# S5 tables: the rotations move from VectorE to GpSimd, and three of the four store streams change the engine that sends them

## The reference, cut to what matters

```python
lam_re = jnp.minimum(A_re, -1e-4); lam_im = A_im; dt = jnp.exp(log_dt)[:, None]
mag = jnp.exp(lam_re * dt)
ab_re, ab_im = mag * jnp.cos(lam_im * dt), mag * jnp.sin(lam_im * dt)   # one step of the state
...
_, _, st_re, st_im = lax.associative_scan(_cplx_op, (a_re, a_im, bu_re, bu_im), axis=1)
y = einsum('gcn,bsgn->bsgc', C_re, st_re) - einsum('gcn,bsgn->bsgc', C_im, st_im)
```

```python
def conv_ffn(xn, w_up, conv_w, conv_b, w_down):
    h = causal_dwconv(xn @ w_up, conv_w, conv_b)
    gate, val = jnp.split(h, 2, axis=-1)
    return (jax.nn.silu(gate) * val) @ w_down
```

## Time and profile before

| | |
|---|---|
| time, median of 3 runs | 2796.97 us (2796.58 to 2798.2) |
| the profiled execution's own time | 2796.79 us |
| its span in the trace | 2795.1 us |
| PE busy / DVE / ACT / POOL | 2632.7 / 1346.1 / 930.6 / 822.1 us |
| table building, group 1 | about 1177 to 1278 us |
| table building, group 2 | about 1386 to 1486 us |

### The profile page before, as it was taken

How to read it: one execution, slowest core, us unless ns; L and a number is a source line. 1 busy time by engine, 2 the same in 40 slices (tenths; PEclk the granted TensorE clock), 3 DMA queues, 4 the chain that set the end, 5 groups by cost and what they waited for, 6 DMA issues and landing times.

```text
span 2795.1 us, 35824 instructions
## 1 busy us (share of the span) xinstructions
PE 2632.7 (94%) x13567; PEld 2186.4 (78%) x13567; DVE 1346.1 (48%) x1668; ACT 930.6 (33%) x1420; POOL 822.1 (29%) x685
## 2 busy tenths in 40 slices
PE   6999799999699999989989999969999999999998
PEld 5778588877587887778778888958878888888886
DVE  5441376776434555674674445642334413431443
ACT  3442354544433312233233344322232312321333
POOL 4222233342322222362362221132222222222221
PEclk8999899999899999999999999989999999999998
DMA  2111000000012211142142124631111111111112
GB/s 90 42 45 49 16 1 1 1 1 1 16 52 57 57 45 49 49 151 95 49 153 92 45 76 154 212 98 49 49 42 49 45 52 46 49 49 49 49 45 83
DMA packets 239923, 164.57 MB, mean 59 GB/s; under 512 B 23981, under 2 KB 227271, under 8 KB 237767
## 3 DMA queue, kind: packets, MB, share of 16 engines
q1 hardware_dynamic: 227648, 149.76, 17.7%
q10 hardware_dynamic: 12167, 13.35, 1.4%
HBM read 129.51 MB, written 29.36 MB: 57 GB/s over the span
## 4 chain that ended last, share of the span: by engine, by line
PE 55%; issue 8%; DVE 4%; POOL 3%; DMA 2%; ACT 1%; ACTq 0%; POOLq 0%; SPq 0%; DVEq 0%
PE acc_o L1556 48%; PE acc_o L1805 3%; POOL dense_lo L374 2%; DMA s_states<-t_hx 2%; DVE t_hx L2430 1%; PE bank_b L2719 1%; PE bank_a L2696 1%; DVE t_tmp L2224 1%; DVE t_rot L2224 0%; POOL c_lo L2560 0%; DVE val L2040 0%; POOL t_mg L2376 0%; DVE t_rot L2407 0%; DVE t_rot L2406 0%; PE acc_o L2108 0%
## 5 line engine op out<-in xcount | busy, mean ns | idle before, releaser
L374 POOL TENSOR_TENSOR dense_lo<-dense_raw,dense_hi 128x512 fp32r<-128x512 f32 x324 | 428.0, 1321 | 1274.2 <-ACT dense_hi L367 1272.9
L367 ACT CAST dense_hi<-dense_raw 128x512 fp32r<-128x512 f32 x324 | 191.4, 593 | 765.5 <-PE acc_o L1556 713.3
L1556 PE MATMUL acc_o<-a_hi,dense_hi 128*128 128x512 f32 x1328 | 414.6, 393 | 8.2 <-POOL a_lo L2566 4.6
L1556 PE MATMUL acc_o<-a_lo,dense_hi 128*128 128x512 f32 x1328 | 410.8, 391 | 0.0
L1556 PE MATMUL acc_o<-a_hi,dense_lo 128*128 128x512 f32 x1328 | 410.4, 390 | 0.0
L1556 PE MATMUL acc_o<-c_hi,dense_hi 128*128 128x512 f32 x1096 | 341.1, 392 | 26.7 <-POOL dense_lo L374 24.5
L1556 PE MATMUL acc_o<-c_lo,dense_hi 128*128 128x512 f32 x1096 | 338.4, 390 | 0.0
L1556 PE MATMUL acc_o<-c_hi,dense_lo 128*128 128x512 f32 x1096 | 338.1, 390 | 0.0
L1556 PEld LDWEIGHTS acc_o<-a_hi,dense_hi 128*128 128x128 f32 x1328 | 248.3, 189 | 61.3 <-POOL a_lo L2566 5.8
L1556 PEld LDWEIGHTS acc_o<-a_lo,dense_hi 128*128 128x128 f32 x1328 | 250.7, 189 | 52.7
L1556 PEld LDWEIGHTS acc_o<-a_hi,dense_lo 128*128 128x128 f32 x1328 | 250.4, 189 | 52.3
(11 more groups left out here) (382 smaller groups left out, 3778.2 us busy)
## 6 DMA issues: line engine op xcount, KB each, us to landing
dense_raw<-in_f_w_up SPq DMA_DIRECT2D x176, 256.0 KB, 3.0
dense_raw<-in_f_w_down SPq DMA_DIRECT2D x72, 256.0 KB, 2.9
w_raw_e<-in_e_w_in SPq DMA_DIRECT2D x44, 256.0 KB, 2.9
s_states<-t_hx ACTq DMA_DIRECT2D x16, 512.0 KB, 3.9
g_in<-s_inputs SPq DMA_DIRECT2D x8, 1024.0 KB, 5.2
hx<-s_states SPq DMA_DIRECT2D x8, 1024.0 KB, 5.3
dense_raw<-in_o_w_glu SPq DMA_DIRECT2D x32, 256.0 KB, 2.8
s_inputs<-t_in SPq DMA_DIRECT2D x14, 512.0 KB, 3.9
```

Of the source, the lines that this page charges most:

```text
L367: nc.scalar.copy(self.hi[:, par, 0:n, :], self.raw[:, par, 0:n, :]).then_inc(w_hi_done, 1)
L374: pool.tensor_tensor(self.lo[:, par, 0:n, :], self.raw[:, par, 0:n, :], self.hi[:, par, 0:n, :].bitcast(F32), op=ALU.subtract).then_inc(w_ ...
L1556: last = nc.tensor.matmul(acc[:, h * HALF:(h + 1) * HALF], w[:, chunk, j, :], x[:, k + j, h * HALF:(h + 1) * HALF], start=first, stop=final)
```

## The change

Rotations are made by POOL (`turns_pool`), one after each up unit of tiles 1 to 4 of groups 1 and 2, into two buffers in turn. SP sends them behind the weight loads of the units that follow. ACT sends the input tables and filters at the end of `half_act`. DVE keeps `t_hx` and `t_mh`. The same transfers of the same sizes are made; `t_tmp` and the second `t_rot` lie elsewhere in SBUF.

```diff
         def load_sp(self, sp):
-            def keep(g, c):
-                n0 = (g - 1) * DT
-                if 0 <= c - 4 < DT:
-                    self.tables.keep_filters_sp(sp, n0 + c - 4)
...
-                elif self.builds(g - 1):
-                    for m in range(2):
+                elif self.builds(g):
+                    for m in range(n):
                         for half in range(2):
                             self.load_up(sp, g, m, half)
-                            keep(g - 1, DT + 2 * m + half)
...
+                            if m > 1:
+                                self.tables.keep_turns_sp(sp, (g - 1) * DT + 2 * m - 4 + half)
...
                 if self.builds(g):
-                    for c in range(2, DT):
-                        self.dn.load(sp, w, n, bass.ds(c * P, P), self.down_unit(g) + c, 0)
-                        keep(g, c)
...
+                    for half in range(2):
+                        self.tables.keep_turns_sp(sp, (g - 1) * DT + DT - 2 + half)
...
         def lo_pool(self, pool):
...
+                if self.builds(g):
+                    for m in range(1 if self.builds(g - 1) else 0, n):
+                        for half in range(2):
+                            self.dn.take_lo(pool, DT, m * 2 + (self.up_unit(g) + half), 0)
+                            if m:
+                                self.tables.turns_pool(pool, (g - 1) * DT + 2 * m - 2 + half)
...
                         if m == n - 1 and self.builds(g):
-                            self.tables.turns_dve(dve, n0)
                             self.tables.powers_dve(dve, n0)
...
-    t_rot = at("t_rot", [P, 2, 2, N5], X_AT)
+    t_rot = [at(f"t_rot{s}", [P, 2, 2, N5], where) for s, where in enumerate((X_AT, Z_AT))]
...
             if n % DT < DT - 1:
                 self.powers_dve(dve, n + 1)
-                self.turns_dve(dve, n + 1)
...
+        def turns_pool(self, pool, n):
...
+            if n == 0:
+                pool.wait_ge(s5_clear, 23)
+            if n > 1:
+                pool.wait_ge(t_turns_out[n % 2], 16 * (n // 2))
+            for o, a, b in ((turn[0], cos, far_cos), (tmp[0], sin, far_sin), (turn[1], sin, far_cos), (tmp[1], cos, far_sin)):
+                pool.tensor_tensor(o, a, b, op=ALU.mult).then_inc(t_turned, 1)
+            pool.wait_ge(t_turned, 6 * n + 4)
+            pool.tensor_tensor(turn[0], turn[0], tmp[0], op=ALU.subtract).then_inc(t_turned, 1)
+            pool.tensor_tensor(turn[1], turn[1], tmp[1], op=ALU.add).then_inc(t_turned, 1)
+            pool.wait_ge(t_turned, 6 * n + 6)
+
+        def keep_turns_sp(self, sp, n):
+            i, two = n // 2, slice(2 * (n % 2), 2 * (n % 2) + 2)
+            sp.wait_ge(t_turned, 6 * n + 6)
+            sp.dma_start(d_turns[i, :, two, :], t_rot[n % 2][:, :, :, :].rearrange("p q k n -> p q (k n)")).then_inc(t_turns_out[n % 2], 16)
...
         def states_dve(self, dve, n):
             if n:
                 dve.wait_ge(t_pe, 4 * n)
-                dve.wait_ge(t_states_out, 32 * n)
+                dve.wait_ge(t_states_out, 16 * n)
...
             nc.scalar.copy(t_fir[:, :, 1, :], self.k1[:, :, :]).then_inc(t_kept, 1)
+            self.keep_filters(act, n)
...
-            act.dma_start(d_turns[i, :, two, :], t_rot[:, :, :, :].rearrange("p q k n -> p q (k n)")).then_inc(t_states_out, 16)
...
+        def keep_filters(self, act, n):
             i, two = n // 2, slice(2 * (n % 2), 2 * (n % 2) + 2)
-            sp.wait_ge(t_kept, 11 * n + 11)
...
+            act.wait_ge(t_kept, 11 * n + 11)
+            act.dma_start(d_inputs[i, :, two, :], self.inputs(n)[:, :, :]).then_inc(t_filters_out, 16)
+            act.dma_start(d_filters[i, :, two, :], t_fir[:, :, :, :].rearrange("p q a n -> p q (a n)")).then_inc(t_filters_out, 16)
```

More of the change, by code:

```diff
@@ L1841, in load_sp @@
                 if self.builds(g):
-                    for c in range(2, DT):
-                        self.dn.load(sp, w, n, bass.ds(c * P, P), self.down_unit(g) + c, 0)
-                        keep(g, c)
[L1845 to L1848, removed]
+                    for half in range(2):
+                        self.tables.keep_turns_sp(sp, (g - 1) * DT + DT - 2 + half)
+                with sp.Fori(1, DT // 2) as i:
+                    for s in range(2):
+                        self.dn.load(sp, w, n, bass.ds(i * (2 * P) + s * P, P), i * 2 + (self.down_unit(g) + s), 0)
         def lo_pool(self, pool):
@@ L1855, in lo_pool @@
                     self.dn.take_lo(pool, DT, self.up_unit(g) + 1, 0)
-                with pool.Fori(1 if self.builds(g - 1) else 0, n) as m:
-                    for half in range(2):
-                        self.dn.take_lo(pool, DT, m * 2 + (self.up_unit(g) + half), 0)
+                if self.builds(g):
[4 more added lines that the diff above has]
+                                self.tables.turns_pool(pool, (g - 1) * DT + 2 * m - 2 + half)
+                else:
+                    with pool.Fori(1 if self.builds(g - 1) else 0, n) as m:
+                        for half in range(2):
+                            self.dn.take_lo(pool, DT, m * 2 + (self.up_unit(g) + half), 0)
                 self.pair_lo(pool, g, 0)
@@ L2130, in trunk @@
     c_s5 = at("c_s5", [P, 2, S5_PAIRS, 16], X_AT + 2 * TILE)
-    t_tmp = at("t_tmp", [P, 2, 2, N5], Z_AT)
+    t_tmp = at("t_tmp", [P, 2, 2, N5], E_AT + 4992)
     t_fir = at("t_fir", [P, 2, 2, P], Z_AT + 2048)
@@ L2155, in trunk @@
     s_act, s_arg, c_kept = sem("s_act"), sem("s_arg"), sem("c_kept")
-    t_pool, t_dve, t_pe, t_kept, t_states_out, t_filters_out = (
-        sem("t_" + n) for n in "pool dve pe kept states_out filters_out".split())
+    t_pool, t_dve, t_pe, t_kept, t_states_out, t_filters_out, t_turned = (
+        sem("t_" + n) for n in "pool dve pe kept states_out filters_out turned".split())
+    t_turns_out = [sem(f"t_turns_out{s}") for s in range(2)]
     V = {n: small[:, k, :] for k, n in enumerate(
@@ L2399, in turns_dve @@
             far_cos, far_sin = (coarse[:, k, pr, :].unsqueeze(3).to_broadcast(step) for k in range(2))
-            turn = [t_rot[:, :, k, :].rearrange("p q (a b) -> p q a b", b=16) for k in range(2)]
+            turn = [t_rot[n % 2][:, :, k, :].rearrange("p q (a b) -> p q a b", b=16) for k in range(2)]
             tmp = [t_tmp[:, k, :, :].rearrange("p q (a b) -> p q a b", b=16) for k in range(2)]
-            if n:
-                dve.wait_ge(t_states_out, 32 * n)
[L2404 to L2407, removed]
+            if n == 0:
[12 more added lines that the diff above has]
+            sp.dma_start(d_turns[i, :, two, :], t_rot[n % 2][:, :, :, :].rearrange("p q k n -> p q (k n)")).then_inc(t_turns_out[n % 2], 16)
         def powers_dve(self, dve, n):
@@ L2491, in keep_states @@
             act.wait_ge(t_dve, 4 * n + 4)
[L2492 removed]
             act.dma_start(d_states[i, :, two, :].rearrange("p q (a x) -> p (q a) x", a=2),
                           t_hx[:, :, :, 1:K9, :].rearrange("p q a k c -> p (q a) (k c)")).then_inc(t_states_out, 16)
[L2496 removed]
+        def keep_filters(self, act, n):
             i, two = n // 2, slice(2 * (n % 2), 2 * (n % 2) + 2)
[L2498 to L2500 removed]
+            act.wait_ge(t_kept, 11 * n + 11)
+            act.dma_start(d_inputs[i, :, two, :], self.inputs(n)[:, :, :]).then_inc(t_filters_out, 16)
+            act.dma_start(d_filters[i, :, two, :], t_fir[:, :, :, :].rearrange("p q a n -> p q (a n)")).then_inc(t_filters_out, 16)
         def wait_kept(self, eng, n):
[L2504 removed]
+            eng.wait_ge(t_states_out, 16 * n)
             eng.wait_ge(t_filters_out, 32 * n)
@@ L2618, in _ @@
                 dn.wait_unit(sp, u_in - 1, 1)
-                sp.wait_ge(t_states_out, 32 * HALVES)
+                sp.wait_ge(t_states_out, 16 * HALVES)
+                sp.wait_ge(t_turns_out[0], 8 * HALVES)
+                sp.wait_ge(t_turns_out[1], 8 * HALVES)
                 sp.wait_ge(t_filters_out, 32 * HALVES)
```

5 lines of the change are left out of this document (removed).

## The result

The changed kernel takes 2760.6 us, median of 4 runs (2760.0 to 2762.14), against 2797.48 us for the kernel before (4 runs, 2796.58 to 2798.2): a ratio of 0.9869, interval 0.9852 to 0.9886. The gain is 36.9 us, and the forecast was 2760.

What follows compares the result with a forecast made beforehand. PE bounds the kernel except in the two table stages, where it waits on a loop through DVE and a DMA landing. 17.7 + 16.5 + 2.6 - 0.5 = 36.3 us off 2796.8 gave 2760, range 2756 to 2772.

Steps and rivals of the forecast that it cites:

- table stage, group 1: Down projection of group 1: 19.4 us lost by PE, all but 1.7 taken back, 17.7 us.
- table stage, group 2: Down projection of group 2: 18.2 us lost by PE, all but 1.7 taken back, 16.5 us.
- start of the two down projections: Last up tile: without six rotations ahead of DVE's scale, PE's 1.3 us wait goes in each group, 2.6 us.
- meeting of POOL and DVE: Up projection, after gate units: rotations meet `val<-gate,val`, delaying POOL's subtraction; 0.5 us lost in all, bounds 0 and 3.4.
- The ring: Table stages: DVE's loop through `t_hx`, its landing and the rotations, 12 to 14 us, falls to 6.3 to 9.8.
- The turn at PE's own pace: Table stages: one unrestrained unit of five k tiles and its half takes PE 9.76 us.
- The first turn: Start of each table stage: stays at 11.48 us, 1.72 over, as POOL's table instructions precede the small subtraction.
- The landing of `t_hx`: Table stages: DMA landing of 3.2 to 5.8 us, within a loop that no longer binds, or barely.
- Rival 1: Table stages: the next ring binds through `t_hx`'s landing, turn 10.8 us, 2772; range 2766 to 2778, chance 0.26.
- ACT's two issues: Table stages: ACT sends input tables and filters, about 0.5 us each, covered by PE's unit; price zero.
- Rival 3: Up projection: rotations hold up `dense_lo` beyond 6.9 us; slower than before at 4.6 us a tile; chance 0.04, shared.
- The room of POOL in the table stage: Table stages: POOL's own work in a turn sums to 8.4 us, 9.3 at the longest, under PE's 9.76.

Runs made afterwards that it cites:

- R = 3: The changed kernel with POOL making the four products of each rotation three times, outputs unchanged: 2796.96 us, ratio 0.9998.
- R = 2: The changed kernel with POOL making the four products of each rotation twice, outputs unchanged: 2767.15 us, ratio 0.9891.

## Why the prediction was right

The two traces are laid side by side by the lag of after against before at the same instruction; its steps are the terms. The lag falls by 1.40 us at the start of the down projection of group 1 and by 17.78 in its table stage, (1275.19 - 1177.69) in the earlier trace rows less 1258.39 - 1178.67 here. Then by 1.35 and 16.59 in group 2, where after has 1368.71 and 1448.42. Below is PE's timeline of the changed kernel: first the start of the stage of group 2, then the first rows of the last half of either stage, which end the two stretches:

```profile
1368.71 0.47 PE L1556 MATMUL acc_o<-c_hi,dense_hi 128*128 128x512 f32 x1 [0.91 <-POOL dense_lo L374]
```

```profile
1258.39 0.38 PE L2449 MATMUL bank_a<-ident,t_gx 128*128 128x128 f32 x2
...
1448.42 0.27 PE L2449 MATMUL bank_a<-ident,t_gx 128*128 128x128 f32 x1
```

| term | predicted | measured |
|---|---|---|
| table stage, group 1 | 17.7 | 17.8 |
| table stage, group 2 | 16.5 | 16.6 |
| start of the two down projections | 2.6 | 2.75 |
| meeting of POOL and DVE | -0.5 | -0.3 at most |
| sum | 36.3 | 36.9 (medians; these rows sum to 36.8) |

- **The ring.** It was the landing of `t_hx` ahead of the rotations. The second buffer alone, with all work left on DVE, gave 27.2 us, so this is shown. The forecast did not say how the two parts of the cure divide: some three quarters are the wait, the rest comes with taking the work off DVE.
- **The turn at PE's own pace.** 9.76 us from one row of before, 9.74 in every turn after the first. The clock came back with the wait, as the windows show.
- **The first turn.** 11.48 us before and after, to the hundredth.
- **The landing of `t_hx`** was bounded by 3.2 to 5.8 us and is 3.0 in the median, 4.6 at most (2.9/3.0/4.6 from issue to landing). Rival 1 needed it long. It got shorter, since rotations are gone from its burst (with the tables back on SP it is 3.0 us as well), and there is spare time around it: DVE waits 1.66 us for PE ahead of `t_hx`.
- **POOL's `t_gx`** ends at 1200.40 + 3.59 = 1203.99, 4.1 us after PE begins the unit behind its half (1199.89), inside the 5 us that the forecast named as the limit.
- **Rotations on POOL** were taken at 4.0 us for six. The products take 0.62 us and the two sums 0.74. One rotation, the meeting and what comes of it, in the timelines of POOL and DVE:

```profile
1122.43 0.62 POOL L2405 TENSOR_TENSOR t_rot<-fine,coarse 128x256 f32<-128x256 f32 x1
...
1125.57 0.74 POOL L2408 TENSOR_TENSOR t_rot<-t_rot,t_tmp 128x256 f32<-128x256 f32 x1
...
1129.24 1.74 POOL L374 TENSOR_TENSOR dense_lo<-dense_raw,dense_hi 128x512 fp32r<-128x512 f32 x1 [2.93 <-ACT dense_hi L367]
```

```profile
1125.85 1.54 DVE L2050 TENSOR_TENSOR val<-gate,val 128x1024 f32<-128x1024 f32 x1
```

  The rotation ends at 1126.31, 3.9 us after it began. `val<-gate,val` takes 1.54 us where the earlier trace rows have 1.23: it was held up for 0.3 us by the rotation's last instruction, still running when it started. The subtraction then ends at 1130.98 and PE starts its unit at 1131.18 without idle time. The slack, 0.51 us in the earlier trace rows, is 0.20. The meeting that I priced at 0.5 us is there, is 0.3 us long, and the slack swallows it. The period of a tile is 21.79 us after and 21.76 before, by DVE's scales of two successive tiles, and 8 x 0.03 us is 0.24.
  By the Trainium skill, page "SBUF — State Buffer", section "Who interferes with whom", each excludes the other for a whole instruction. The rows agree that it works in both directions (`val<-gate,val` 1.54 us against 1.23, a product on POOL 1.60 against 0.62), but the strict price of 3.4 us was not paid, since only the last, short instruction of POOL was in the way.
- **ACT's two issues** cost nothing, as said, and not for the whole reason given. The unit on PE covers them, and with the rotations off the ring either sender will do. But the edit shortens the landing of `t_hx`, and on the kernel before this was worth 5 us. The forecast had weighed the issues' time and not what the transfers leave free.
- **Rival 3** was priced at 4.6 us a tile for a loss, six instructions in 11.5 us. The experiment with R = 3, 8.8 us undisturbed, already gave all of it back. So the room up to the crossing was over-priced: I had let PE pay a us for each us of POOL, and meetings with DVE and the clock after the waits come on top. With the two meetings those 8.8 us are 10.7, 3.8 over the 6.9 us of room, and the tile pays 5.0 for them. With R = 2 PE's waits rise by 13.0 - 7.2 = 5.8 us and the medians by 6.6: behind waits of 0.8 us the granted clock stays at 1.00. With R = 3 the waits rise by 24.0 us and the medians by 36.4.
- **The room of POOL in the table stage** was put at 8.4 of 9.76 us. Twice the `t_mg`, 2.4 us more undisturbed, made the turn 2.4 us longer. The room was 0.8 us, not 1.4. POOL's busy time in a turn is even less than the sum had it, 1.29 + 2.39 + 3.59 + 0.56 = 7.83 us, but the sum left out that POOL, too, waits in this loop, 1.23 us for ACT's rounding. The forecast stood because nothing was added there, but it stood closer to the edge than its text had it.

What stays open is small. The profiled execution of after starts with a loss of 2.4 us to the kernel before, and the granted clock of its first 60 us is 0.69 against 0.86; nothing of the change is there. In the later stages it wins another 1.8 us, spread over a thousand us. The two nearly cancel, and no experiment here was made on either.

## What to carry to other kernels

When a buffer's release is a DMA landing and the wait for it stands on a busy engine, the whole queue of that engine waits, and a second buffer is worth more than the move of the work (27 of 37 us here). Price a ring by its turn on the engine that has none to spare, from one unrestrained turn in the trace; take the clock that comes back with the wait as part of it. Work added to a helper engine is cheap until it reaches the wait that the bound engine hangs on, and from there a us cost more than a us here (5.0 for 3.8 in a tile with R = 3): the room to fill is the helper's idle time, less the part of it that it spends waiting inside the same loop.

## What the hardware showed that I had not expected

- A wait of PE can cost more than its length: 4.23 us of it were followed by 7.2 us at a granted clock of 0.60, 3.17 us by 5.5 us at 0.69 (from 1139.5 in the kernel with R = 3), and 2.51 us in the changed kernel by 7 us at 0.76. Waits of 0.9 to 1.5 us in the changed kernel left the clock at 1.00. In between it went both ways: in the kernel with `t_mg` made twice, waits of 2.14 and 2.23 us left it at 1.00 (1212.3 to 1219, 1224.6 to 1231), and another of 2.23 us was followed by 0.76 (1236.8 to 1244).
- On POOL, an add or subtract of 128 x 256 with plain operands takes 0.74 us, longer than the product of the same size with broadcast operands, 0.62 us.
- A product of 0.62 us on POOL that meets DVE takes 1.60 us: the delay, 0.98 us, is longer than the product itself. DVE's `val<-gate,val`, 1.23 us alone, had started 0.19 us before the one at 1131.09.
- The landing of the same 512 KB (`t_hx`) took 5.07 us in the burst of the earlier trace rows, 3.3 in the median when the tables had left ahead of it, and 3.0 in the changed kernel, where the tables leave only 1.2 us and more ahead of it (issues at 1192.48 and 1193.68) but no rotation is sent between. It is 3.0 us too where the tables come from SP and the rotations are made on POOL.
- Moving work off an engine does not free its whole time: `t_mh` on DVE, the same 64 instructions, took 34.1 us before and 45.5 after.
